# The later heads' queries in four pieces of 272 columns instead of two of 512 and one of 32

## What is computed

```python
qry = (xb @ peer_query).reshape(P, PEER_HEADS, 2, PEER_KEY_DIM)
scores = jnp.einsum('phsd,hsnd->phsn', qry, keys)         # 2 x 128 scores for a frame and head
top_s, top_i = lax.top_k(scores, PEER_TOPK)               # 16 best of each half
cand = top_s[:, :, 0, :, None] + top_s[:, :, 1, None, :]  # 256 sums
best_s, best_c = lax.top_k(cand.reshape(...), PEER_TOPK)  # 16 experts of 16384
gate = jax.nn.softmax(best_s, axis=-1)
u_rows = peer_down[expert]                                # 16 rows of 1024 for each frame and head
act = jax.nn.gelu(jnp.einsum('pd,ped->pe', xb, u_rows))
v_rows = peer_up[expert]                                  # 16 more rows of 1024
out = jnp.einsum('pe,ped->pd', gate * act, v_rows)
```

## Time and profile before

| | |
|---|---|
| median of 3 runs | 1677.19 us (1674.56 to 1678.44) |
| the profiled execution | 1672.85 us, its span 1671.1 us |
| PE busy | 1419.8 us (85%) |
| DVE busy | 1178.5 us (71%) |
| ACT busy | 504.4 us (30%) |
| POOL busy | 729.8 us (44%) |
| gathers' queue, share of 16 DMA engines | 82.5% |
| mean granted clock of PE | 0.934 |

### The profile page before, as it was taken

The page is one execution under the profiler, slowest core; times in us unless marked ns, Lnnn a source line. Parts: engine busy times, 40 slices in busy tenths (PEclk is TensorE's granted clock), DMA queues, the critical chain, the costliest instruction groups (busy, mean ns, idle before and its releaser), DMA issues.

```text
span 1671.1 us, 14832 instructions
## 1 busy us (share of the span) xinstructions
PE 1419.8 (85%) x4373; PEld 685.7 (41%) x4373; DVE 1178.5 (71%) x2555; ACT 504.4 (30%) x1607; POOL 729.8 (44%) x623
## 2 busy tenths in 40 slices
PE   7999999899798789788987898789878987767843
PEld 6744465555344334333433343334333433322311
DVE  2897858875876777677767776677777777767755
ACT  2111212432333333233333333333333333333332
POOL 1003714454444454454445454444544444454452
PEclk9999999999899999899999998899999999999876
DMA  6202307999999999999999999999999999999997
GB/s 238 101 1 65 143 30 298 365 421 421 421 421 421 421 422 420 421 422 421 406 423 421 420 406 422 421 421 414 420 422 384 413 422 421 421 422 421 422 421 293
DMA packets 85328, 606.22 MB, mean 363 GB/s; under 512 B 11008, under 2 KB 11520, under 8 KB 13568
## 3 DMA queue, kind: packets, MB, share of 16 engines
q0 software_dynamic: 78336, 570.46, 82.5%
q1 hardware_dynamic: 6912, 34.81, 5.6%
HBM read 601.97 MB, written 2.88 MB: 362 GB/s over the span
## 4 chain that ended last, share of the span: by engine, by line
PE 40%; DMA 33%; DVE 14%; issue 4%; DVEq 3%; POOL 3%; ACT 3%; ACTq 0%; POOLq 0%; SPq 0%
DMA arena<-experts,expert 32%; PE ps L1546 25%; PE ps L1504 6%; DVE arena L1201 5%; PE ps L1407 4%; DVE region_b L942 3%; DVEq L1085 3%; POOL arena L550 2%; PE ps L1395 2%; PE ps L1476 1%; ACT weight L788 1%; PE ps L1384 1%; ACT late L799 1%; DVE cst L1181 0%; DVE cst L1178 0%
## 5 line engine op out<-in xcount | busy, mean ns | idle before, releaser
L1546 PE MATMUL ps<-arena,late 128*128 128x512 f32 x2016 | 960.9, 634 | 179.0 <-ACT late L799 178.8
L550 POOL DMA_INDIRECT arena<-experts,expert x544 | 659.6, 1212 | 724.3 <-PE ps L1546 599.2
L1201 DVE CUSTOM_DVE_ANT_0 arena<-arena,hn 128x1024 f32<-128x1024 f32 x544 | 655.1, 1223 | 357.8 <-DMA arena<-experts,expert 351.1
L1546 PEld LDWEIGHTS ps<-arena,late 128*128 128x128 f32 x2016 | 400.9, 203 | 721.7 <-issue 560.0
L785 ACT ACTIVATE gl<-dots 128x4 f32<-128x4 f32 (+1 forms) x139 | 28.5, 205 | 800.9 <-DVE dots L1201 800.8
L799 ACT ACTIVATE late<-cst,weight 128x128 f32<-128x128 f32 (+1 forms) x536 | 169.1, 385 | 9.7 <-issue 0.3
L788 ACT ACTIVATE weight<-gl,gate 128x1 f32<-128x1 f32 x544 | 116.0, 283 | 9.5
L1407 PE MATMUL ps<-arena,hT 128*128 128x512 f32 x256 | 111.7, 595 | 0.0
L1504 PE MATMUL ps<-hT,region_b 128*128 128x512 f32 x224 | 98.4, 592 | 0.0
L942 DVE SCALAR_TENSOR_TENSOR region_b<-region_b,par 128x574 f32<-128x574 f32 x120 | 92.5, 813 | 4.9 <-issue 0.4
L1407 PEld LDWEIGHTS ps<-arena,hT 128*128 128x128 f32 x256 | 48.6, 192 | 58.5 <-issue 58.4
(11 more groups left out here) (156 smaller groups left out, 863.4 us busy)
## 6 DMA issues: line engine op xcount, KB each, us to landing
arena<-weights SPq DMA_DIRECT2D x8, 2048.0 KB, 11.6
region_b<-head_weights SPq DMA_DIRECT2D x8, 1152.0 KB, 9.5
arena<-experts,expert POOLq DMA_INDIRECT x544
xs<-x_prompt SPq DMA_DIRECT2D x4, 512.0 KB, 5.6
y_prompt<-xs SPq DMA_DIRECT2D x4, 512.0 KB, 4.3
cst<-consts SPq DMA_DIRECT2D x1, 836.0 KB, 21.7
hn<-gain_ffn SPq DMA_DIRECT2D x1, 512.0 KB, 3.9
region_b<-gain_ffn SPq DMA_DIRECT2D x1, 512.0 KB, 3.7
```

The costliest lines, as they stand in the source:

```text
L550: pool.indirect_dma_start(rows_of(n), None, experts, bass.IndirectOffsetOnAxis(ap=expert[:, vt % BUFS, k:k + 1], axis=0))\
L1201: last = v.tensor_tensor_reduce(out=rows_of(n)[:, 0:D], in0=rows_of(n)[:, 0:D], in1=hn[:, tile_of(vt)], scale=1.0, scalar=0.0, op0=ALU.mul ...
L1546: last = mm(ps[:, 2 * (vt % 2) + half, :], diag[:, n % DIAGS, :], rows_of(n)[:, D + half * SEC:D + (half + 1) * SEC], start=k == first * G ...
```

## The change

A later head's queries now come in four pieces that are alike: piece i is half i // 2 of the query with 272 of the 544 columns (the sample's are the last 32), 8 matmuls each, in PSUM banks 4 to 7. In tile m = 0 of the head before, PE has one piece behind each of the four groups; the scores keep their place behind group 2 of m = 1. ACT copies pieces 0 to 2 behind its groups 1 to 3 of m = 0 and piece 3 behind group 0 of m = 1. For head 1, PE has a piece ahead of each group of tile 2, as it had for three of them before, and the scores move from ahead of group 3 to behind it; ACT's copies of pieces now stand ahead of groups 0 to 3 instead of behind groups 0 to 2. The first head's sample queries are no longer 16 matmuls of their own: the fourth tile's have 160 columns instead of 128.

```diff
-PROJ = 6
+PIECES = 4
+PROJ = PIECES + 3
@@ plan()
-    return order + query(3) + sums(1, 0) + keys(3) + query(4) + sums(1, 1) + keys(4) + sums(1, 2) + sums(1, 3)
+    return order + query(3) + sums(1, 0) + keys(3) + sums(1, 1) + keys(4) + sums(1, 2) + sums(1, 3)
+def asked_with(t):
+    return P + DEC if t == HT - 1 else P
@@ ACT
             def later_query(head, i):
                 act.wait_ge(s_proj, (head - 1) * PROJ + (i + 1))
-                if i < 2:
-                    dst, src = queryT[:, i, 0:SEQ], ps[:, Q_BANKS + i, :]
-                else:
-                    dst = queryT[:, :, SEQ:T]
-                    src = ps[:, Q_BANKS + 2, 0:2 * DEC].rearrange("p (s t) -> p s t", s=2)
-                nc.scalar.activation(dst, src, ACT.Copy).then_inc(s_queries, 1)
+                s, half = i // 2, i % 2
+                nc.scalar.activation(queryT[:, s, half * HALF:(half + 1) * HALF], ps[:, Q_BANKS + i, 0:HALF], ACT.Copy)\
+                    .then_inc(s_queries, 1)
...
-            first_query(4)
             group(1, 2)
             group(1, 3)
             softmax(3)
+            later_query(1, 0)
             group(2, 0)
-            later_query(1, 0)
+            later_query(1, 1)
             group(2, 1)
-            later_query(1, 1)
+            later_query(1, 2)
             group(2, 2)
-            later_query(1, 2)
+            later_query(1, 3)
             group(2, 3)
...
-                    return {0: {1: lambda: later_query(head + 1, 0), 3: lambda: later_query(head + 1, 1)},
-                            1: {1: lambda: later_query(head + 1, 2), 3: lambda: later_scores(head + 1)}}.get(m, {})
+                    return {0: {g + 1: lambda g=g: later_query(head + 1, g) for g in range(3)},
+                            1: {0: lambda: later_query(head + 1, 3), 3: lambda: later_scores(head + 1)}}.get(m, {})
@@ PE
             def later_query(head, i):
...
+                s, half = i // 2, i % 2
+                for k in range(KD):
+                    last = mm(ps[:, Q_BANKS + i, 0:HALF], weights[:, k, s * KEYS:(s + 1) * KEYS],
+                              hT[:, k, half * HALF:(half + 1) * HALF], start=k == 0, stop=k == KD - 1)
                 last.then_inc(s_proj, 1)
...
                 if m == 0:
-                    return {0: lambda: later_query(head + 1, 0), 2: lambda: later_query(head + 1, 1)}
+                    return {g: lambda g=g: later_query(head + 1, g) for g in range(PIECES)}
                 if m == 1:
-                    return {0: lambda: later_query(head + 1, 2), 2: lambda: later_scores(head + 1)}
+                    return {2: lambda: later_scores(head + 1)}
...
             later_query(1, 2)
             sum_up(2, 2)
+            later_query(1, 3)
+            sum_up(2, 3)
             later_scores(1)
-            sum_up(2, 3)
             head_tile(3, {})
```

More of the change, by code:

```diff
@@ L200 @@
 ret_yT.2 ffn_t.1.0 ffn_t.1.1 ret_qT.4 ret_kT.4 query.1 ret_yT.3 ret_yT.4 ffn_t.2.0 ffn_t.2.1 query.2 ffn_t.3.0
-ffn_t.3.1 ffn_t.4.0 ffn_t.4.1 query.3 query.4
+ffn_t.3.1 ffn_t.4.0 ffn_t.4.1 query.3
 """)}
@@ L726, in first_query @@
             def first_query(t):
-                r = ROWS[t]
                 filled(("query", t))
-                src = bank(("query", t))[:, 0:2 * P].rearrange("p (s t) -> p s t", s=2)[:, :, 0:r]
-                emptied(("query", t), nc.scalar.activation(first_queryT[:, t % 2, :, 0:r], src, ACT.Copy))
+                width = asked_with(t)
+                src = bank(("query", t))[:, 0:2 * width].rearrange("p (s t) -> p s t", s=2)
+                last = nc.scalar.activation(first_queryT[:, t % 2, :, 0:P], src[:, :, 0:P], ACT.Copy)
+                if width > P:
+                    last = nc.scalar.activation(first_queryT[:, SAMPLE % 2, :, 0:DEC], src[:, :, P:width], ACT.Copy)
+                emptied(("query", t), last)
             def later_query(head, i):
                 act.wait_ge(s_proj, (head - 1) * PROJ + (i + 1))
-                if i < 2:
-                    dst, src = queryT[:, i, 0:SEQ], ps[:, Q_BANKS + i, :]
-                else:
-                    dst = queryT[:, :, SEQ:T]
-                    src = ps[:, Q_BANKS + 2, 0:2 * DEC].rearrange("p (s t) -> p s t", s=2)
-                nc.scalar.activation(dst, src, ACT.Copy).then_inc(s_queries, 1)
+                s, half = i // 2, i % 2
+                nc.scalar.activation(queryT[:, s, half * HALF:(half + 1) * HALF], ps[:, Q_BANKS + i, 0:HALF], ACT.Copy)\
+                    .then_inc(s_queries, 1)
             def later_scores(head):
@@ L748, in later_scores @@
                 for s in range(2):
-                    act.wait_ge(s_proj, (head - 1) * PROJ + (4 + s))
+                    act.wait_ge(s_proj, (head - 1) * PROJ + (PIECES + 1 + s))
                     src = ps[:, Q_BANKS + s, :].rearrange("p (t n) -> p t n", t=HT)
@@ L1475, in first_query @@
                     for k in range(KD):
-                        last = mm(out[:, s * P:s * P + r], head_w[0][0][:, k, s * KEYS:(s + 1) * KEYS],
-                                  hT[:, k, t * P:t * P + r], start=k == 0, stop=k == KD - 1)
+                        last = mm(out[:, s * width:(s + 1) * width], head_w[0][0][:, k, s * KEYS:(s + 1) * KEYS],
+                                  hT[:, k, t * P:t * P + width], start=k == 0, stop=k == KD - 1)
                 done(last)
             def first_scores(t):
-                pe.wait_ge(s_by["act"], EMPTIED[("query", t)])
+                pe.wait_ge(s_by["act"], EMPTIED[("query", min(t, HT - 1))])
                 out = open_bank(("scores", t))
@@ L1495, in later_query @@
                 if head == 1:
-                    pe.wait_ge(s_by["act"], EMPTIED[("query", SAMPLE)])
+                    pe.wait_ge(s_by["act"], EMPTIED[("query", HT - 1)])
                     pe.wait_ge(s_by["dve"], EMPTIED[("scores", SAMPLE)])
+                elif i < 3:
+                    pe.wait_ge(s_scored, (head - 2) * 3 + (i + 1))
                 else:
-                    pe.wait_ge(s_scored, (head - 2) * 3 + (i + 1))
+                    pe.wait_ge(s_queries, (head - 1) * PIECES)
                 pe.wait_ge(s_hw[head % 2], 16 * (head // 2 + 1))
[L1501 to L1510, removed]
+                s, half = i // 2, i % 2
+                for k in range(KD):
+                    last = mm(ps[:, Q_BANKS + i, 0:HALF], weights[:, k, s * KEYS:(s + 1) * KEYS],
+                              hT[:, k, half * HALF:(half + 1) * HALF], start=k == 0, stop=k == KD - 1)
                 last.then_inc(s_proj, 1)
@@ L1515, in later_scores @@
                 for i in range(3):
-                    pe.wait_ge(s_queries, (head - 1) * 3 + (i + 1 if i < 2 else 3))
+                    pe.wait_ge(s_queries, (head - 1) * PIECES + 2 * min(i + 1, 2))
                     out = ps[:, Q_BANKS + i, :]
```

4 lines of the change are left out of this document (2 added, 2 removed).

## The result

| | before | changed |
|---|---|---|
| median | 1675.88 us (4 runs, 1673.65 to 1678.44) | 1687.51 us (4 runs, 1686.75 to 1688.60) |
| the profiled execution, its span | 1672.85, 1671.1 us | 1687.94, 1686.1 us |
| mean granted clock of PE | 0.934 | 0.935 |

The ratio is 1.0069, with a 95% interval of 1.0056 to 1.0082. Predicted were 1671.5 us and a faster kernel; the time lies outside the range. Ratios here leave out one run of 2352.44 us, of the kernel with one round of the loop, whose granted clock was 0.556 where the other ten had 0.93 or more.

The account below looks back on a forecast made before the run. The prediction took the DMA's gathers to bound the kernel from about 350 us: 1672.85 - 7.5 + 4 = 1669.4 us for the profiled execution, and 1671.5 us with half of the median's 4.3 us carried over; range 1664.5 to 1680.

Parts of the forecast that it names:

- the term -7.5: Heads 3 to 6, m = 0: DMA dry spells losing 8.2 us would close but for some 0.7 us.
- The cover that I counted: Bytes asked for and not yet moved when a gather is issued; 0 at 1290.75, 5.6 us at head 1's gather.
- the dry spells stay: Rival, heads 3 to 6: dips come from the gathers' rows, not slots freed late; only head 1's loss remains, 1681; chance 0.05.
- +4 us: Head 1, tile 2: group, piece, copy and next weights close a loop; a gather delayed 5.2 us outlasts its cover.
- 4.3 less 0.4: Head 1's gather at 442.12: DMA loss when a 5.2 us delay leaves 0.4 us of cover.
- The copy, 0.40 us; from the gelu to the first diagonal 1.6; a piece 3.71: Head 1, tile 2: durations on ACT and PE that, with a group, make a round of 12.7 us.
- The group in the loop, 6.87 us: Head 1, tile 2: PE's time for each group of sums within a 12.7 us round.
- Group 0 starts at 371.6: Tile 2 on PE: first group's start, after piece 0, its copy and the table load on ACT.
- Group 3 at 409.3: Tile 2 on PE: last group's start, after three rounds of 12.55 to 12.7 us.
- DVE waits about 9 us: Head 1: sign of being right, DVE's wait for the scores at `top_first(4)`, before 3.02 us.
- One hole near 450 us, behind what DVE has queued: Head 1: the DMA dips there as tile 3's group 2 and its gather, queued behind DVE, come 5.2 us late.
- the loop at the lower clock throughout: Rival, tile 2: each of four groups takes 3.2 us more, making a 17 us hole, 1684.5 us; chance 0.08.

Follow-up runs that it names:

- the kernel with one round of the loop: Changed kernel with ACT's head 1 copies back behind tile 2's groups, except piece 1 copied ahead of group 1; 1676.09 us, ratio 0.9991 to the kernel before.
- A kernel with hardly any pieces: Changed kernel with head 1's copies behind the groups, and query pieces of heads 2 to 7 cut to one of eight matmuls; 1674.68 us, ratio 0.9990.
- the first experiment: Changed kernel with only ACT's copies of head 1's pieces put back behind the groups of tile 2; 1675.19 us, ratio 0.9999 to the kernel before.
- The loop alone: Kernel before, with only ACT's three copies of head 1's pieces moved ahead of groups 0 to 2 of tile 2; 1684.88 us, ratio 1.0058.
- The loop with the new pieces and the scores ahead: Changed kernel with head 1's scores back ahead of group 3 of tile 2 on PE, copies still ahead of groups; 1682.43 us, ratio 1.0037.

## Why the prediction was wrong

Two terms of the sum 1672.85 - 7.5 + 4 failed.

**"Against 421 they lose ... together 8.2 us" (the term -7.5).** This step failed in kind. I took a stretch's mean rate below 421 for lost time. The landings go on at their pace through the largest of these dips. The rows that I had the earlier trace rows were read rightly: POOL did wait for PE, and the gather was issued late. The change even did what the forecast asked of it. POOL's wait ahead of the same gather, number 400, fell from 8.14 to 4.94 us (from 7.94 to 4.72 ahead of number 208, the one at 799.64):

```profile
1302.26 0.95 POOL L556 DMA_INDIRECT arena<-experts,expert  x1 [4.94 <-PE ps L1548]
```

The time didn't follow, because at these places the landings didn't hang on it. The bytes "asked for and not yet moved" were near zero at 1290.75, but the gathers already asked for were not done: the bytes had gained a lead of 6.3 us over the landings since landing 80. The cover that I counted, in bytes over all 16 engines, leaves that lead out. A kernel with hardly any pieces has the same 1281.5 us from landing 37 to 540. The rival *the dry spells stay* had a chance of 0.05 and the wrong reason: they moved rather than stayed. Those around 800 and 965 did close, by the page's slices 19 to 24, while others came at 1138 and 1265 to 1349 us (401, 412, 405); it made no difference either way, 1171.0 us against 1171.7.

**"+4 us" for head 1.** The mechanism was right and each link of it is in the rows: the copy ahead of the weights, PE idle for ACT each round, the scores late, DVE behind them. The size was off by a factor of three: 11.7 us by the landings, 11.6 by the medians. The price itself, 4.3 less 0.4, was that of the dip at 1290.75, which cost nothing; at head 1 there was no lead of bytes, and idle time of the DMA had its full price. The steps below it:

- *The copy, 0.40 us; from the gelu to the first diagonal 1.6; a piece 3.71*: measured 0.40, 1.6 (392.19 to 393.8) and 3.66 from start to start. Right.
- *The group in the loop, 6.87 us*: wrong. Behind an idle time of 2 to 3.5 us three of four groups took 8.6 to 8.7 us from start to start, and the granted clock was 0.83 in two of the four stretches of 10 us from 390, 1.00 in the others. The group behind the same 1.97 us that fell into such a stretch of 1.00 took 6.97. Two of the three rounds are 14.4 and 14.5 us and not 12.7. I had the rows for this (8.83 behind 2.10 us) and put them into the rivals, since most groups elsewhere stay near 7.15.
- *Group 0 starts at 371.6*: it started at 379.39, 7.8 us later. Of this 3.3 us is the late start of the execution, 2.9 us the last group of tile 1 being late besides (363.67, forecast 357.5; DVE waits for a landing at 360.76 where it was 354.65), and 1.5 us that group's own length (8.4 us).
- *Group 3 at 409.3*: 421.07. The 11.8 us are those 7.8 and 4.0 from the rounds. Before it started at 406.67, so I had the loop put it 2.6 us off; it is 14.4, or 11.1 without the late start.
- *DVE waits about 9 us*: 18.12.
- *One hole near 450 us, behind what DVE has queued*: wrong place. The slots that PE's groups free inside the loop came late already, and I priced none of them, because by my durations they were at most 2.6 us off. The first gathers behind the groups went out at 398.29, 410.56 and 425.79 where it was 388.17, 399.51 and 409.68 before: 6.8, 7.8 and 12.8 us later, the late start taken off. The cover I reckoned with was 5.6 us. So the DMA is short from 390 on and stands still at 424.

The rival *the loop at the lower clock throughout* (0.08, 1684.5 us) was the nearest: its place, its cause and its hole of 17 us. The measured loss is 12, and three of four groups took the longer time.

**What held.** PE's price for the pieces (3.66 us each); the 272-column copy; that ACT's extra copies in the later heads, the 160-column query and the moved weights cost nothing together: the first experiment is level with before with all of them in it.

**Which part costs what.** The loop alone costs 9.4 us in the kernel before (1684.88 against 1675.49), 7.3 by the landings of its profiled execution. The loop with the new pieces and the scores ahead costs 6.9 us (1682.43 against 1675.49), and the scores behind it another 5.

**What stays open.** Whether one engine lags, and which. And what the steps are: of the 1281.5 us of before from landing 37 to 540, 503 gathers at 2.485 us are 1250, and the weights of the five heads loaded in that time, 1.18 MB each, some 14. The other 17 are the steps, 18 of about 0.95 us in this kernel. A packet of the instruction queue q14 stands within 8 us ahead of each of them in the DMA view, but the other 19 of its 37 packets have no step of their own, and no run here moved one. The steps would be the next thing to look into, not PE's order.

## What to carry to other kernels

When the bound is a stream of transfers, find something that shows each one land, number the landings and compare those of two kernels: the difference of two numbers says how much was lost and between which, and the mean rate doesn't. Compare too the bytes moved with the bytes landed: a dip costs nothing as long as it only uses up a lead of the bytes, as the one at 1290 us did, and costs its length where there is none. A rate that falls to the share of one engine hints at the first, a rate of zero at the second.

Before an operation that waits for PE is put ahead of the work that PE waits for next, even one of 0.4 us on an idle engine, add up the round that it closes, and price PE's part by the rows behind an idle time of that size. Then write down for each group of the round when it starts now and would start then, and set each delay against the cover, before anything that lies further behind.

## What the hardware showed that I had not expected

The mean rate of the 16 DMA engines fell to 293 GB/s over 14 us, with 2 us at 23 to 47, and five gathers of 1.049 MB still landed in 12.51 us, since the bytes moved had run 2.7 MB ahead of the gathers landed. The landings slipped by 0.9 to 1.0 us at the same 16 gather numbers in twelve kernels that differ in PE's and ACT's order. And 120 us of matmuls without use on PE raised the mean granted clock from 0.935 to 0.955 and cost no time in a kernel that is bound by transfers.
